# A two-layer hybrid mixer with dense and routed FFN: norm factors applied behind the products, tokens turned by halves, last down products summed in PSUM

## What is computed

```
h = rms_norm(x, norm1_w)           # x * rsqrt(mean(x*x) + 1e-6) * w
z = h @ w_in                       # 8968 columns, split into q, k, v, gates
x = x + mixer(z) @ w_out           # retention, dilated attention, mLSTM; sigmoid gates
h = rms_norm(x, norm2_w)
layer 0:  x = x + (silu(h @ w_gate) * (h @ w_up)) @ w_down       # inner width 2816
layer 1:  x = x + sum over top-2 of 8 experts, inner width 3584, after softmax of h @ w_router + b
```

## Time and profile before

| | us |
|---|---|
| three runs | 1884.96, 1881.33, 1886.08 (median 1884.96) |
| profiled execution | 1884.84 |
| its span, first to last instruction | 1882.9 |
| mean granted clock of TensorE | 0.973 |
| busy: PE, DVE, ACT, POOL | 1815.4, 1406.5, 1105.9, 34.1 |

### The profile page before, as it was taken

The page is one execution under the profiler, slowest core; times in us unless marked ns, Lnnn a source line. Parts: engine busy times, 40 slices in busy tenths (PEclk is TensorE's granted clock), DMA queues, the critical chain, the costliest instruction groups (busy, mean ns, idle before and its releaser), DMA issues.

```text
span 1882.9 us, 23630 instructions
## 1 busy us (share of the span) xinstructions
PE 1815.4 (96%) x8718; PEld 1519.3 (81%) x8718; DVE 1406.5 (75%) x1199; ACT 1105.9 (59%) x990; POOL 34.1 (2%) x31
## 2 busy tenths in 40 slices
PE   6999998999989999987999999999999999999998
PEld 5788887788878888867888888888888888888886
DVE  5767467455567674764988989889899898898995
ACT  3436553433334464633776777767677777677774
POOL 0002000000000010000000000000000000000000
PEclk8999999999979999996999999999999999999999
DMA  6444346464334543471998999989989999899993
GB/s 229 157 169 137 130 145 246 157 200 148 121 112 157 178 151 118 141 252 62 362 378 307 396 332 349 393 309 386 377 305 398 325 353 394 305 391 356 320 399 143
DMA packets 215266, 484.38 MB, mean 257 GB/s; under 512 B 7473, under 2 KB 11825, under 8 KB 215089
## 3 DMA queue, kind: packets, MB, share of 16 engines
q1 hardware_dynamic: 215216, 483.70, 70.8%
HBM read 482.62 MB, written 1.05 MB: 257 GB/s over the span
## 4 chain that ended last, share of the span: by engine, by line
PE 92%; DVE 4%; ACT 2%; DMA 1%; issue 1%; POOL 0%; SPq 0%; POOLq 0%; DVEq 0%; ACTq 0%
PE ps L523 28%; PE ps L525 28%; PE ps L524 28%; PE ps L528 6%; PE ps L532 3%; DVE sb_wlo L312 1%; DMA sb_ringa<-in_w_in_dram 1%; ACT sb_whi L305 0%; DVE sb_hlo L1335 0%; DVE sb_w L1318 0%; DVE sb_hlo L1334 0%; ACT sb_w L997 0%; DMA sb_small<-in_small_dram 0%; DVE sb_z L1392 0%; DVE sb_x L1664 0%
## 5 line engine op out<-in xcount | busy, mean ns | idle before, releaser
L341 DVE TENSOR_TENSOR sb_wlo<-sb_z,sb_whi 128x2048 fp32r<-128x2048 f32 x334 | 755.5, 2289 | 99.3 <-ACT sb_whi L335 98.1
L335 ACT ACTIVATE sb_whi<-sb_z 128x2048 fp32r<-128x2048 f32 x333 | 633.0, 1922 | 201.3 <-PE ps L525 201.2
L523 PE MATMUL ps<-sb_whi,sb_hhi 128*128 128x512 f32 (+1 forms) x1744 | 692.2, 397 | 13.9 <-DVE sb_hlo L1334 7.1
L524 PE MATMUL ps<-sb_whi,sb_hlo 128*128 128x512 f32 (+1 forms) x1744 | 680.4, 390 | 0.0
L525 PE MATMUL ps<-sb_wlo,sb_hhi 128*128 128x512 f32 (+1 forms) x1744 | 680.2, 390 | 0.0
L523 PEld LDWEIGHTS ps<-sb_whi,sb_hhi 128*128 128x128 f32 x1744 | 332.3, 191 | 86.2 <-DVE sb_hlo L1334 8.0
L525 PEld LDWEIGHTS ps<-sb_wlo,sb_hhi 128*128 128x128 f32 x1744 | 332.0, 190 | 69.1
L524 PEld LDWEIGHTS ps<-sb_whi,sb_hlo 128*128 128x128 f32 x1744 | 333.1, 191 | 63.9
L312 DVE TENSOR_TENSOR sb_wlo<-sb_ringa,sb_whi 128x2048 fp32r<-128x2048 f32 (+1 forms) x90 | 200.8, 2240 | 83.4 <-ACT sb_whi L305 82.9
L305 ACT ACTIVATE sb_whi<-sb_ringa 128x2048 fp32r<-128x2048 f32 (+1 forms) x90 | 168.5, 1877 | 156.6 <-DMA sb_ringa<-in_w_in_dram 81.2
L523 PE MATMUL ps<-sb_whi,sb_ahi 128*128 128x512 f32 x568 | 222.6, 392 | 1.0 <-DVE sb_alo L1334 1.0
(11 more groups left out here) (206 smaller groups left out, 1085.2 us busy)
## 6 DMA issues: line engine op xcount, KB each, us to landing
sb_z<-in_moe_w_gate_dram SPq DMA_DIRECT2D x112, 1024.0 KB, 7.2
sb_z<-in_moe_w_up_dram SPq DMA_DIRECT2D x112, 1024.0 KB, 7.5
sb_z<-in_moe_w_down_dram SPq DMA_DIRECT2D x112, 1024.0 KB, 7.2
sb_ringa<-in_w_in_dram SPq DMA_DIRECT2D x68, 1024.0 KB, 4.8
sb_z<-in_ffn_w_gate_dram SPq DMA_DIRECT2D x10, 1024.0 KB, 5.2
sb_z<-in_ffn_w_up_dram SPq DMA_DIRECT2D x10, 1024.0 KB, 6.1
sb_z<-in_ffn_w_down_dram SPq DMA_DIRECT2D x10, 1024.0 KB, 4.9
sb_ringa<-in_w_out_dram SPq DMA_DIRECT2D x8, 1024.0 KB, 4.9
```

The source lines that it names most:

```text
L335: nc.scalar.activation(e_lane(s)[0], ringb[:, s % RING_B, :], ACT.Copy).then_inc(hi_done, 1)
L341: nc.vector.tensor_tensor(lo, ringb[:, s % RING_B, :], hi.bitcast(F32), ALU.subtract).then_inc(split, 1)
L523: nc.tensor.matmul(out, lh, rh, start=start, stop=False)
L524: nc.tensor.matmul(out, ll, rh, start=False, stop=False)
```

## The change

- `scale_tokens` and `normalise` are gone. x itself is turned, unscaled. The factor of a token is applied where a result leaves PSUM with tokens on partitions: `z_copy` becomes two `tensor_scalar`, one per tile; `gate_out` and `f_silu` get the factor as ACT's scale; `f_mult` becomes `scalar_tensor_tensor`; `z8` and the router's logits too.
- The convolution's output has tokens along the free dimension. For it PE multiplies an all-ones matrix by two diagonal matrices of the factors (`root_row`), DVE copies the row and multiplies instead of copying.
- Tokens are turned by halves, each half between two product slots. In phase A, z product 0's first half (slot 1) stands between the two convolution products (slots 0 and 2), and the gate columns stand behind its second half (slot 3). In phase B, layer 0, the first four slots come as up half 0, gate half 0, gate half 1, up half 1. In layer 1 the router's matmuls are done in two halves.
- x is loaded in two halves, the second behind the first weight slot, and the constants behind slot 3; an early ACT operation loads its table.
- The last full down chunk and the short last chunk of a half go into one PSUM sum: two sums fewer per token tile, and the first half of the next layer's tokens is turned before the last short slot.
- For the gather x times the factor is still written to `w1t`, now behind the turning.

The diff, cut to its core:

```diff
-F_SUMS = 2 * F_TILES
+F_SUMS = 2 * TT * F_CHUNKS
...
+        diag, rrow = w2[:, 0:TT * P].rearrange("p (t n) -> p t n", t=TT), w2[:, S:2 * S]
...
+            sp.dma_start(x[:, :, 0:C], xin[:, :, 0:C]).then_inc(x_in, 16)
...
                 for h in range(2):
-                    load(layer, "A", h, part(w_in, KH * h, KH, IN_QK, C))
+                    load(layer, "A", 2 * h, part(w_in, KH * h, KH, IN_QK, C))
+                    if layer == 0 and h == 0:
+                        sp.dma_start(x[:, :, C:], xin[:, :, C:]).then_inc(x_rest, 16)
+                    load(layer, "A", 2 * h + 1, part(w_in, KH * h, KH, 0, C))
                 if layer == 0:
                     sp.dma_start(const[:, P:], a["const"][:, P:]).then_inc(consts_in, 16)
...
-            return 2 * (q % 3) if q < N_LOOP else 2 * (q % 2)
+            return 4 - 2 * (q % 3) if q < N_LOOP else 2 * (q % 2)
+        def turn_bank(n, b):
+            return 6 + b % 2 if n % 3 == 0 else 4 + b
...
+                def root_row():
+                    pe.wait_ge(diag_ok, L)
+                    for t in range(TT):
+                        m = mm(ps[:, 7, t * P:(t + 1) * P], ones, diag[:, t, :])
+                    m.then_inc(rrow_mm, 1)
...
+                conv_chunk(0)
+                if layer == 0:
+                    pe.wait_ge(x_rest, 16)
+                else:
+                    pe.wait_ge(d_out, F_SUMS)
+                turn_tokens(x, 3 * layer, ht_turned, (2, 3))
                 z_chunk(0, 0)
+                conv_chunk(1)
+                if layer == 0:
+                    pe.wait_ge(consts_in, 16)
+                root_row()
                 z_chunk(0, 1)
+                gate_columns()
+                pe.wait_ge(conv_pad, L)
                 pe.wait_ge(z8_sb, L)
...
-                pe.wait_ge(tok_ready, 2 * (3 * layer + 3))
-                turn_tokens(w1t, ht_turned)
+                        if half == 1 and kh == 0:
+                            pe.wait_ge(x_half, 2 * layer + 1)
+                            turn_tokens(x, 3 * layer + 2, ht_turned, (0, 1))
                 pe.wait_ge(ht_lo, 4 * (3 * layer + 2) + 2)
...
-                    f_gate(0, 0)
-                    f_up(2, 0)
+                    f_first(0, 2, 0, True)
+                    turn_rest()
+                    f_first(1, 0, 0, True)
+                    pe.wait_ge(ht_lo, 4 * 3)
+                    f_first(2, 0, 1, False)
+                    f_first(3, 2, 1, False)
...
-                    f_down(s + 4, F_CHUNKS - 1)
-                    f_turn(F_CHUNKS, n=HALF // P)
-                    f_down(s + 6, F_CHUNKS, k=HALF // P)
+                    f_last(s + 4, 0, 0, (ahi, alo), 0, 4, True)
+                    f_turn(F_CHUNKS, n=kl)
+                    f_last(s + 4, 1, 0, (ahi, alo), 0, 4, True).then_inc(used, 1)
+                    pe.wait_ge(a_lo, F_TILES)
+                    for t in range(TT):
+                        m = f_last(s + 5, t, 0, (hhi, hlo), KD - kl, kl, False)
+                    m.then_inc(used, 1)
+                    for t in range(TT):
+                        m = f_last(s + 6, t, 1, (ahi, alo), 0, 4, True)
+                    m.then_inc(used, 1)
+                    pe.wait_ge(d_out, F_SUMS - 2)
+                    turn_tokens(x, 3, ht_turned, (0, 1))
+                    for t in range(TT):
+                        m = f_last(s + 7, t, 1, (hhi, hlo), KD - kl, kl, False)
...
+                turned_lo(3 * layer, norm1, (2, 3))
                 lo_a(2)
+                dve.wait_ge(rstd_ok, 2 * layer + 1)
+                for t in range(TT):
+                    m = V.tensor_scalar(diag[:, t, :], ident, rstd2[:, t:t + 1], None, ALU.mult)
+                m.then_inc(diag_ok, 1)
                 lo_a(3)
+                dve.wait_ge(rrow_mm, L)
+                link(V.tensor_copy(rrow, ps[:, 7, 0:S]))
+                wait_used(dve, layer, "A", 2)
+                V.tensor_tensor(w4a[:, :, TAPS - 1:], ps[:, 0:4, 0:S],
+                                rrow.unsqueeze(1).to_broadcast([P, 4, S]), ALU.mult).then_inc(conv_pad, 1)
                 lo_a(4)
...
-                    V.tensor_copy(dst, ps[:, pair(q):pair(q) + 2, 0:n]).then_inc(z_out, 1)
+                    for t in range(TT):
+                        dst = z[:, t, c:c + n] if isinstance(r, int) else z[:, t, bass.ds(r * (3 * C) + c, n)]
+                        m = V.tensor_scalar(dst, ps[:, pair(q) + t, 0:n], rstd2[:, t:t + 1], None, ALU.mult)
+                    m.then_inc(z_out, 1)
...
+                x_add(0)
+                lo_of(dve, layer, "B", 0)
+                turned_lo(3 * layer + 2, norm2, (0, 1))
+                lo_of(dve, layer, "B", 1)
+                x_add(1)
+                total()
```

More of the change, by code:

```diff
@@ L397, in _ @@
                 for h in range(2):
-                    load(layer, "A", h, part(w_in, KH * h, KH, IN_QK, C))
+                    load(layer, "A", 2 * h, part(w_in, KH * h, KH, IN_QK, C))
+                    if layer == 0 and h == 0:
+                        sp.dma_start(x[:, :, C:], xin[:, :, C:]).then_inc(x_rest, 16)
+                    load(layer, "A", 2 * h + 1, part(w_in, KH * h, KH, 0, C))
                 if layer == 0:
                     sp.dma_start(const[:, P:], a["const"][:, P:]).then_inc(consts_in, 16)
-                for s in range(4):
-                    load(layer, "A", 2 + s, part(w_in, KH * (s % 2), KH, s // 2 * C, C))
+                for h in range(2):
+                    load(layer, "A", 4 + h, part(w_in, KH * h, KH, C, C))
                 with sp.Fori(0, (N_LOOP - 2) // 3) as i:
@@ L421, in _ @@
                     gu, wd = (a["ffn_w_gate"][0], a["ffn_w_up"][0]), a["ffn_w_down"][0]
-                    for s in range(4):
-                        load(0, "B", s, part(gu[s // 2], KH * (s % 2), KH, 0, C))
+                    for s, (m, h) in enumerate(((1, 0), (0, 0), (0, 1), (1, 1))):
+                        load(0, "B", s, part(gu[m], KH * h, KH, 0, C))
                     for s in range(4):
@@ L437, in _ @@
                     for h in range(2):
-                        load(0, "B", s0 + 4 + h, part(wd, 4 * (F_CHUNKS - 1), 4, h * C, C))
-                    for h in range(2):
-                        load(0, "B", s0 + 6 + h, part(wd, 4 * F_CHUNKS, HALF // P, h * C, C), k=HALF // P)
+                        load(0, "B", s0 + 4 + 2 * h, part(wd, 4 * (F_CHUNKS - 1), 4, h * C, C))
+                        load(0, "B", s0 + 5 + 2 * h, part(wd, 4 * F_CHUNKS, HALF // P, h * C, C), k=HALF // P)
                 else:
@@ L831, in f_down, with f_first, f_last @@
                             product(0, "B", s + h, r, (6 - 2 * h, 7 - 2 * h), (ahi, alo), 0, True, True, k=k)
-                    f_gate(0, 0)
-                    f_up(2, 0)
+                    def f_first(s, bank, h, first):
+                        product(0, "B", s, 0, (bank, bank + 1), (hhi, hlo), KH * h, first, not first)
+                    def f_last(s, t, h, lhs, rows0, k, first):
+                        wait_lo(pe, 0, "B", s)
+                        ln = lane(0, "B", s)
+                        hi, lo = (w[:, ln, 0:k * C].rearrange("p (k n) -> p k n", k=k) for w in (whi, wlo))
+                        for kk in range(k):
+                            m = mm3(ps[:, 6 - 2 * h + t, :], lhs[0][:, rows0 + kk, t * P:(t + 1) * P],
+                                    lhs[1][:, rows0 + kk, t * P:(t + 1) * P], hi[:, kk, :], lo[:, kk, :],
+                                    first and kk == 0, not first and kk == k - 1)
+                        return m
+                    f_first(0, 2, 0, True)
[4 more added lines that the diff above has]
+                    f_first(3, 2, 1, False)
                     f_gate(4, 1)
@@ L1385, in _ @@
                 dve.wait_ge(z8_mm, L)
[L1386 removed]
+                for t in range(TT):
+                    m = V.tensor_scalar(z8[:, t, :], ps[:, 6, t * 8:t * 8 + 8], rstd2[:, t:t + 1], None, ALU.mult)
+                m.then_inc(z8_sb, 1)
                 def z_copy(q, r=0):
```

241 lines of the change are left out of this document (132 added, 109 removed).

## The result

The changed kernel takes 1851.77 us (median of four runs, 1850.58 to 1856.72), the one before, run beside it, 1883.14 (four runs, 1880.93 to 1886.08). The ratio is 0.9837, 95% interval 0.9812 to 0.9862; 31 us are gone where 30 were forecast. A second measurement on another chip gave 1853.0 against 1881.32, ratio 0.9855 (0.9835 to 0.9876).

A forecast was written before the change was run, and what follows sets the result against it. TensorE, 96% busy, bounds the kernel, with about 67 us idle; 5.6-0.5+6.8+13.4-2.2+7.5 = 30.6, less 0.1 and 0.5, gives 30: 1855 us from 1884.84. Range 1849 to 1862, over all cases 1843 to 1868.

The forecast's parts named there:

- A: Start through layer 0's third z product: first product at 11.5, third z product 60.7 instead of 66.29; 5.6 us won, 0.5 back.
- ACT is free at 7.3: Start, layer 0: eight transposes and last two high parts done, ScalarE free at 7.3 us to split the first weight slot.
- E: End of convolution product 1 in each layer; forecast at 31.7 us in layer 0 (was 34.8), 541.1 in layer 1.
- gap of 5 to 6 us: Before the third z products: PE done by E+22.7, then waits 5 to 6 us where it waited 2.17 and 0.83.
- my own sign: Forecast check: PE waits 5 to 6 us for a low part before the third z product in both layers.
- Rival 1: Third z products: PE takes everything back, VectorE's queue gets through first, they start at E+22.7; total 1841 us, chance 0.13.
- split z copy: Z copies become two scalings of 512: 1.29 against 1.23 us, 0.06 more, eleven times a layer, claimed hidden.
- B: Norm 2, layer 0: the 8.9 us stretch becomes sixteen transposes of 1.9, slot 4's high part 0.2 late; 6.8 us won.
- C: End of dense FFN to layer 1's third z product: 568.8 instead of 582.24, 13.4 us won, 2.2 back for clock.
- D: Norm 2 and routing, layer 1: 35.3 us become 27.3 with the clock low, 0.5 for slow transposes; 7.5 us won.
- Rival 2: Joints not closed: six half-turnings each wait 1.8 us, total 1866, chance 0.2; argued against by covering products, except in the router.
- Rival 4: Z stages: transposes and the new gap keep the lower clock in force, slower than before, 1895 us; chance 0.03.

The follow-up runs named there:

- x_whole: The changed kernel with x loaded in one transfer ahead of everything, as before the change; 1854.05 us.
- late_turn: The changed kernel with the first half of norm 2's tokens turned behind both output products instead of between them, in both layers; 1860.56 us.
- late_turn_c: The changed kernel with the first half of layer 1's tokens turned behind the last short down slot instead of ahead of it; 1854.67 us.
- gates_first: The changed kernel with the 48 narrow gate matmuls ahead of the second half of z product 0 instead of behind it; 1853.1 us.
- root_wait: The changed kernel with TensorE waiting for the inverse root before the second half of each turning (four places); 1855.01 us.

## Why the prediction was right, point by point

**A, 5.1 forecast, 2.9 measured: right mechanism, the start mis-sized.** The first product came at 13.18, not 11.5. Two steps failed. One is "ACT is free at 7.3" with the weights there: ACT in the timeline, the turned tiles' high parts and the first weight slot's.

```profile
6.40 1.63 ACT L1058 ACTIVATE sb_hhi<-ps,sb_small 128x256 fp32r<-128x256 f32 x4 [4.21 <-PE ps L541]
8.80 1.91 ACT L307 ACTIVATE sb_whi<-sb_ringa 128x2048 fp32r<-128x2048 f32 x1 [0.77 <-DMA sb_ringa<-in_w_in_dram]
```

The transposes came 0.3 later than counted (5.19; forecast 4.9), the high parts ended at 8.03, 0.4 more, and then ACT waited 0.8 for the slot's load: 8.80. The bracket of the forecast, "13.5 if its load is late", was nearer than its 11.5. The other is the term "half of x no longer lies ahead of them, 1.3 to 1.7", of which `x_whole` shows nothing beyond the scatter. From the first product to E passed 20.6 us where 20.2 were counted, so E is 33.7, not 31.7. The chain from E was 29.7, forecast 29.0. The half microsecond set aside for the clock was not needed.

**The gap of 5 to 6 us was there and is not visible.** PE waited 1.79 and 1.85 us at the third z products, which by my own sign would be wrong. In front of the wait lies a stretch at the lower clock (10.2 and 6.8 us) on the gate columns and z product 1, which takes about half its length from PE's slack: 1.8 + 5.1 = 6.9 in layer 0 (6.3 forecast), 1.85 + 3.4 = 5.3 in layer 1 (5.0). Eight profiles of layer 0 with different shares of the two (wait 1.68 to 4.79, stretch 3.4 to 10.2) give 6.5 to 7.4. The end of the chain hardly moves with it: from DVE's copy to the third z product they have 28.8 to 29.6. Rival 1 is out: the chain did not get through earlier.

The chain of layer 1, DVE and ACT in the timeline:

```profile
531.52 0.42 DVE L1452 COPY sb_w<-ps 128x256 f32<-128x256 f32 x1 [4.02 <-PE ps L537]
...
536.49 5.09 DVE L1464 SCALAR_TENSOR_TENSOR sb_w4b<-sb_w4a,sb_small,sb_w4b 128x256 f32<-128x256 f32 x12
543.33 0.36 DVE L1471 TENSOR_SCALAR sb_st<-ps,sb_st 128x8 f32<-128x8 f32 x2 [1.75 <-PE ps L534]
544.50 2.29 DVE L314 TENSOR_TENSOR sb_wlo<-sb_ringa,sb_whi 128x2048 fp32r<-128x2048 f32 x1 [0.81 <-ACT sb_whi L307]
546.71 1.40 DVE L1479 TENSOR_SCALAR sb_z<-ps,sb_st 128x512 f32<-128x512 f32 x2
...
556.71 4.47 DVE L314 TENSOR_TENSOR sb_wlo<-sb_ringa,sb_whi 128x2048 fp32r<-128x2048 f32 x2
```

```profile
541.61 1.06 ACT L1079 ACTIVATE sb_w4b<-sb_w4b 128x1024 f32<-128x1024 f32 x1 [8.86 <-DVE sb_w4b L1464]
542.58 1.89 ACT L307 ACTIVATE sb_whi<-sb_ringa 128x2048 fp32r<-128x2048 f32 x1
```

E is 530.9. The taps end at E+10.7 (forecast 10.5), slot 5's low part at E+15.9 (15.7), from z copy 0 to the next low part 10.0 (9.8), third z product E+28.1 (27.7). The root row, for which no row stood, is four matmuls in 0.36 us, and DVE's copy starts at E+0.6 (0.5 taken).

**A split z copy** takes 1.40 where one copy took 1.23: 0.17 us more, not 0.06. My nearest row, a pair of two-operand products, was not near enough. The Trainium skill (VectorE: DVE Perf Modes, "Side-by-side: where the cycles go for N=2048 bf16") had the better figure: its 150 cycles per instruction gave an estimate of 0.16. One such copy stands on each chain, so this is 0.1 of the 0.7 and 0.4 us by which the chains were longer than forecast.

**B, 6.8 forecast, 6.1 measured.** The failed term is "slot 4's high part now stands behind the first SiLU: by my count 0.2 late". It was 1.55, because the SiLU's table load of 1.28 us is not hidden: ACT had nothing to do for 8.0 us before it, and the load begins when the wait ends. So the term was 1.3 to 1.4 us too small; the rest of the step came 0.6 to 0.7 better than counted, and where is not shown.

**C, 13.4 forecast less 2.2 for a slow stretch; 13.1 measured.** The sum for the end of the FFN stands nearly: from DVE's copy at 548.99 before to its copy at 531.52 now 17.5 are won, of which 10.1 came in, so 7.4, where 7.9 were counted. From the copy on 5.7 were won, where 5.5 were counted. The 2.2 were wrong: no stretch came behind the gap; it came ahead of it, where PE had to wait in any case.

**D, 7.5 forecast, 7.0 measured.** The clock was low in the router (20.5 us from 827.6), as taken. Rival 2's wait is there once, in the router's second half (1.84), as its "except in the router" says; at the other joints it is not, and there `late_turn` and `late_turn_c` bring it.

**Rival 4** is refuted on its own point. Lower-clock time fell from 95.7 to 68.2 us, and from 88.7 to 58.0 in the second pair of profiles. By the page's rule (the Trainium skill, TensorE: Matmul & The Clock Gate, Part 4) transposes between products should not help the clock; in this trace 28 transposes of the tokens and of the FFN's products lie between products from 488 to 535, all at granted clock 1.00. No harm shows from them where full products surround them.

The total came within 0.2% because the misses have both signs: 2.2 and 0.7 too much in A and B and 0.5 in D, 1.9 too little in C, 1.1 and -2.1 between them that no step had: of the 30.6 summed up, 28.1. So part of the agreement is luck. Besides, the profiled execution is 5 us slower than the median of its four runs.

Left open: why the stretches at the lower clock begin and end where they do (the same kernel has them in other places in another execution); and what z product 0's half between the convolution products is worth by itself, which was not tried. No run puts the scaling ahead of the turning again with the halves left in place: what it brings by itself is argued from the 30.7 us of waits that are gone, and from the prices of its parts above.

## What to carry to other kernels

When a normalisation is linear per row, its factor can wait until results leave PSUM; what this brings is that tokens can be turned in halves as soon as they exist, and each half then needs a full product to run behind it (2.2 to 2.5 us where none stood, 1.8 or 2.2 behind narrow matmuls). Then look for the next queue: here two activations stood ahead of a weight's high part on ACT, and moving them cost nothing and brought 4 us more. A wait forecast on PE may hide in a stretch at the lower clock; read the start of the next product against the chain that sets it, not the length of the wait.

## What the runs showed of the hardware that was not expected

POOL's operation for the root, 128 x 2 elements, takes more than ten times as long when it begins while DVE is subtracting two SBUF tiles. POOL and then DVE, in the timeline:

```profile
14.66 2.23 POOL L498 TENSOR_SCALAR sb_root<-sb_st 128x2 f32<-128x2 f32 x1 [13.81 <-DVE sb_st L1402]
...
327.16 2.16 POOL L498 TENSOR_SCALAR sb_root<-sb_st 128x2 f32<-128x2 f32 x1 [64.02 <-DVE sb_st L1402]
...
518.38 0.19 POOL L498 TENSOR_SCALAR sb_root<-sb_st 128x2 f32<-128x2 f32 x1 [188.26 <-DVE sb_st L1402]
```

```profile
14.55 2.29 DVE L314 TENSOR_TENSOR sb_wlo<-sb_ringa,sb_whi 128x2048 fp32r<-128x2048 f32 x1
...
326.99 2.28 DVE L314 TENSOR_TENSOR sb_wlo<-sb_z,sb_whi 128x2048 fp32r<-128x2048 f32 x1
```

The first two end with the subtraction (16.89 and 16.84; 329.32 and 329.27). The third, beside which DVE has nothing to do, takes 0.19. In `gates_first` the first operation, by chance, began 0.04 us before the subtraction. It took 0.19, and the next one, 0.71 long elsewhere (at 16.98 in the changed kernel), took 2.63; POOL, then DVE:

```profile
14.02 0.19 POOL L498 TENSOR_SCALAR sb_root<-sb_st 128x2 f32<-128x2 f32 x1 [13.17 <-DVE sb_st L1402]
14.30 2.63 POOL L500 TENSOR_TENSOR sb_st<-sb_root 128x2 f32<-128x2 f32 x1
```

```profile
14.06 2.29 DVE L314 TENSOR_TENSOR sb_wlo<-sb_ringa,sb_whi 128x2048 fp32r<-128x2048 f32 x1 [0.24 <-ACT sb_whi L307]
```

So whichever of POOL's two operations begins beside the subtraction is held up; the reason is not shown. It is hidden in the changed kernel, since the root has time; in `root_wait` POOL's 2.16 us (from 328.09) are longer than the wait of 0.54 that PE had for the root at norm 2 of layer 0, which at 0.19 would not have been there.
